# Attention branch c: two items a step on TensorE, the pair's second item normalised ahead of the next pair's maximum, the gate's products moved by half a chunk

## The reference, cut to what matters

```python
def block(args):
    qn, qp = args
    sc = (jnp.einsum('bqhd,bkhd->bhqk', qn, k_nope) + jnp.einsum('bqhd,bkd->bhqk', qp, k_pe)).astype(jnp.float32) * scale
    p = jax.nn.softmax(sc, axis=-1).astype(v.dtype)
    return jnp.einsum('bhqk,bkhd->bqhd', p, v)
...
branches = jnp.stack([oa, ob, oc], axis=2)
proj = jnp.einsum('bsnw,nwd->bsnd', branches, w_branch[l])
gates = jax.nn.sigmoid(h @ w_gate[l] + b_gate[l]).reshape(b, s_len, N_BRANCH, D_MODEL)
x = x + jnp.sum(gates * proj, axis=2) @ w_out[l]
```

## Time and profile before

| | us |
| --- | --- |
| median of 3 runs | 4201.57 |
| lowest and highest | 4198.54 and 4201.68 |
| the profiled execution's own time | 4204.7 |
| its span, first to last instruction | 4202.9 |
| branch c in layer 1, first score to the projection's second matmul | 2414.82 to 2506.14 |
| TensorE busy over the span | 3970.8 (94%) |
| VectorE busy over the span | 2298.5 (55%) |
| mean granted clock of TensorE | 0.981 |

### The profile page before, as it was taken

How to read it: one execution, slowest core, us unless ns; L and a number is a source line. 1 busy time by engine, 2 the same in 40 slices (tenths; PEclk the granted TensorE clock), 3 DMA queues, 4 the chain that set the end, 5 groups by cost and what they waited for, 6 DMA issues and landing times.

```text
span 4202.9 us, 52035 instructions
## 1 busy us (share of the span) xinstructions
PE 3970.8 (94%) x17600; PEld 2864.4 (68%) x17600; DVE 2298.5 (55%) x4427; ACT 1439.5 (34%) x3092; POOL 2201.4 (52%) x2879
## 2 busy tenths in 40 slices
PE   9999988887779999989999999999999999999998
PEld 7877633333336666679867768888888867768887
DVE  8376887887866666565375434321331375444321
ACT  3142322222245444445243323322332143323322
POOL 7646643333333333357835637556665735637654
PEclk9999999899899999999999999999999999999999
DMA  5342799999999999965412213333333312313332
GB/s 148 87 112 71 312 427 427 426 427 427 414 426 423 403 424 425 426 228 178 128 41 71 91 48 103 97 93 100 95 97 94 99 41 71 96 46 105 95 95 75
DMA packets 190865, 839.69 MB, mean 200 GB/s; under 512 B 41744, under 2 KB 44480, under 8 KB 125120
## 3 DMA queue, kind: packets, MB, share of 16 engines
q0 software_dynamic: 73728, 536.90, 30.4%
q1 hardware_dynamic: 91904, 293.46, 22.2%
q10 hardware_dynamic: 25024, 6.69, 0.8%
HBM read 831.47 MB, written 4.59 MB: 199 GB/s over the span
## 4 chain that ended last, share of the span: by engine, by line
PE 71%; DMA 13%; DVE 9%; ACT 2%; issue 2%; POOL 2%; DVEq 1%; ACTq 0%; POOLq 0%; SPq 0%
PE bank L953 17%; PE bank L955 17%; PE bank L954 17%; PE bank L1352 8%; DMA rows_o<-in_peer_uv,of_picks_int 4%; DMA row_keys<-in_peer_uv,of_picks_int 2%; DMA rows_x<-in_peer_uv,of_picks_int 2%; POOL wl L780 1%; DVE rows_o L2807 1%; PE bank L1047 1%; DMA work<-in_peer_uv,of_picks_int 1%; DMA rows_w<-in_peer_uv,of_picks_int 1%; DMA row_norm<-in_peer_uv,of_picks_int 1%; PE bank L1385 1%; DMA row_temps<-in_peer_uv,of_picks_int 1%
## 5 line engine op out<-in xcount | busy, mean ns | idle before, releaser
L780 POOL TENSOR_TENSOR wl<-raw,wh 128x256 fp32r<-128x256 f32 (+1 forms) x1032 | 824.7, 830 | 256.4 <-ACT wh L2067 232.1
L953 PE MATMUL bank<-xh,wh 128*128 128x512 f32 (+1 forms) x2304 | 881.3, 383 | 3.3 <-POOL wl L780 3.3
L955 PE MATMUL bank<-xh,wl 128*128 128x512 f32 (+1 forms) x2304 | 862.9, 375 | 0.0
L954 PE MATMUL bank<-xl,wh 128*128 128x512 f32 (+1 forms) x2304 | 862.4, 374 | 0.0
L780 POOL TENSOR_TENSOR wl<-raw_more,wh 128x256 fp32r<-128x256 f32 (+1 forms) x780 | 612.1, 816 | 286.5 <-ACT wh L2067 276.0
L953 PEld LDWEIGHTS bank<-xh,wh 128*128 128x128 f32 x2304 | 434.6, 189 | 105.8 <-issue 28.3
L955 PEld LDWEIGHTS bank<-xh,wl 128*128 128x128 f32 x2304 | 434.6, 189 | 79.3
L954 PEld LDWEIGHTS bank<-xl,wh 128*128 128x128 f32 x2304 | 435.1, 189 | 74.1 <-issue 2.2
L1352 PE MATMUL bank<-rows_o,diag 128*128 128x512 f32 x676 | 330.1, 623 | 48.0 <-ACT diag L2023 47.8
L2865 DVE TENSOR_TENSOR work<-bank,rstd 128x512 f32<-128x512 f32 (+1 forms) x184 | 114.8, 626 | 443.0 <-PE bank L955 442.4
L840 POOL DMA_INDIRECT rows_o<-in_peer_uv,of_picks_int x169 | 167.5, 991 | 288.5 <-PE bank L1352 277.6
(11 more groups left out here) (585 smaller groups left out, 8005.9 us busy)
## 6 DMA issues: line engine op xcount, KB each, us to landing
raw_more<-in_w_l SPq DMA_DIRECT2D x186, 512.0 KB
raw<-in_w_l SPq DMA_DIRECT2D x182, 512.0 KB
raw<-in_w SPq DMA_DIRECT2D x54, 512.0 KB
raw_more<-in_w_l SPq DMA_DIRECT2D x40, 448.0 KB
raw<-in_w_l SPq DMA_DIRECT2D x40, 448.0 KB
raw_more<-in_w_l SPq DMA_DIRECT2D x28, 256.0 KB
raw<-in_w_l SPq DMA_DIRECT2D x28, 256.0 KB
raw<-in_w SPq DMA_DIRECT2D x20, 256.0 KB
```

The source lines that it names most:

```text
L780: last = gp.tensor_tensor(wl[:, slot, c], source[:, c], f32(wh[:, slot, c]), ALU.subtract)
L953: pe.matmul(out, wh[:, slot, c], ah, start=k == 0, stop=False)
L954: pe.matmul(out, wh[:, slot, c], al, start=False, stop=False)
L955: mm = pe.matmul(out, wl[:, slot, c], ah, start=False, stop=k == last)
```

## The change

TensorE's loop takes a pair at a step. Step t has, in this order: turning item 2t-2; the scores of items 2t and 2t+1; the values product, for t = 4, 5, 8, 9; turning item 2t-1; the second half of gate chunk t-1; the first half of gate chunk t. VectorE normalises the odd item of a pair before it takes the next pair's first maximum, where it did so behind it; the rest of its loop is as it was. ScalarE's, GpSimd's and SyncE's programs are unchanged. No instruction is added or taken away: TensorE has 10426 rows and VectorE 2659 in the list of both kernels.

```diff
-                for s in range(18):
-                    if s < 16 and s % 2 == 0:
-                        h, qb = item_c(s)
-                        if s > 1:
-                            pe.wait_ge(exp_ready.sem, exp_ready.at(48 + s, l))
+                def turn_c(i):
+                    pe.wait_ge(prob_ready.sem, prob_ready.at(48 + i + 1, l))
+                    turn_tile(work[:, i % 4, :], l)
+                def values_c(h, turns):
+                    wait_total(l)
+                    pe.wait_ge(turn_read.sem, turn_read.at(t_base + turns, l))
+                    for b in range(NB):
+                        mm = pe.matmul(total[:], vt[:, b, h * P:(h + 1) * P], pt_c[h % 2][:, b, :], start=b == 0, stop=b == NB - 1)
+                    mm.then_inc(summed.sem, 1)
+                for t in range(10):
+                    if 1 <= t <= 8:
+                        turn_c(2 * t - 2)
+                    if t < 8:
+                        h, qb = item_c(2 * t)
+                        if t > 0:
+                            pe.wait_ge(exp_ready.sem, exp_ready.at(48 + 2 * t, l))
                         for m in range(2):
                             pe.matmul(score[m][:], qk[:, h + m, qb * P:(qb + 1) * P], qk[:, 6 + h + m, :], start=True, stop=False)
...
-                    if s < 16:
-                        linear(AT_L["gate_c"], s // 2, l, normed, share=(s % 2, 2))
-                    if s >= 8 and s % 8 < 2:
-                        h = 2 * (s // 8 - 1) + s % 8
-                        wait_total(l)
-                        pe.wait_ge(turn_read.sem, turn_read.at(t_base + s - 1, l))
...
-                    if 1 <= s <= 16:
-                        pe.wait_ge(prob_ready.sem, prob_ready.at(48 + s, l))
-                        turn_tile(work[:, (s - 1) % 4, :], l)
+                    if t in (4, 5, 8, 9):
+                        values_c(2 * (t // 4 - 1) + t % 4, 2 * t - 1 if t % 4 == 0 else 2 * t - 2)
+                    if 1 <= t <= 8:
+                        turn_c(2 * t - 1)
+                    if 1 <= t <= 8:
+                        linear(AT_L["gate_c"], t - 1, l, normed, share=(1, 2))
+                    if t < 8:
+                        linear(AT_L["gate_c"], t, l, normed, share=(0, 2))
...
                 for s in range(18):
+                    if 2 <= s and s % 2 == 0 and s <= 16:
+                        normalise(48 + s - 1, l, (s - 1) % 4, T, False)
                     if s < 16:
                         dve.wait_ge(scored.sem, scored.at(64 + s + 1, l))
...
-                    if 1 <= s <= 16:
+                    if s % 2 == 1 and s < 16:
                         normalise(48 + s - 1, l, (s - 1) % 4, T, False)
```

More of the change, by code:

```diff
@@ L1591, in _ @@
                                       start=False, stop=True).then_inc(scored.sem, 1)
-                    if s < 16:
-                        linear(AT_L["gate_c"], s // 2, l, normed, share=(s % 2, 2))
-                    if s >= 8 and s % 8 < 2:
-                        h = 2 * (s // 8 - 1) + s % 8
-                        wait_total(l)
-                        pe.wait_ge(turn_read.sem, turn_read.at(t_base + s - 1, l))
-                        for b in range(NB):
-                            mm = pe.matmul(total[:], vt[:, b, h * P:(h + 1) * P], pt_c[h % 2][:, b, :], start=b == 0, stop=b == NB - 1)
-                        mm.then_inc(summed.sem, 1)
-                    if 1 <= s <= 16:
-                        pe.wait_ge(prob_ready.sem, prob_ready.at(48 + s, l))
-                        turn_tile(work[:, (s - 1) % 4, :], l)
+                    if t in (4, 5, 8, 9):
[6 more added lines that the diff above has]
+                        linear(AT_L["gate_c"], t, l, normed, share=(0, 2))
                 t0 = use["total"] - 4
```

## The result

The changed kernel takes 4206.85 us, the median of 14 runs (4202.53 to 4216.6), against 4201.32 of the kernel before, run beside it 14 times. The ratio is 1.0015, 95% interval [1.0008, 1.0021]: 5.5 us slower. That is within the 0.2% that the prediction called no change, but it is clear of the noise of these runs, as the interval does not reach 1. The profiled execution took 4210.13 us for a span of 4208.3.

The account below looks back on a forecast made before the run. TensorE's own work was taken to bound the kernel. The terms -1.0, +0.7, +0.2, +2.45 and -1.3 sum to +1.05 us a layer, +2.1 in all, giving 4203.7 us; range 4199 to 4209.

Parts of the forecast that it names:

- The likeliest case: Whole kernel: the summed terms hold, +2.1 us with some tenths either way, no measurable change; chance 0.52.
- fewer runs, 7 pairs: TensorE's gate matmuls in branch c: one run of 24 replaces two of 12, -0.14 us a pair, -1.0 a layer.
- turnings slip: Branch c: normalising meets GpSimd's tile split, so TensorE's turning comes 0.17 us later in 4 steps, +0.7 a layer.
- first step: First pair of branch c: only half a chunk covers normalising item 0, so its turning waits, +0.2 us a layer.
- gap: Step 5: TensorE waits to turn item 9, whose normalising stands behind head_out of head 1, +2.45 us a layer.
- end: End of branch c: the last half chunk covers the wait before head 3's values, -1.3 us a layer.
- The chain at the end of a step: VectorE's gate sum, second maximum and normalising of item 2t precede TensorE's turning; meeting GpSimd makes normalising 0.80 us, +0.7 a layer.
- The whole-operation wait: Rival: VectorE's normalising waits until GpSimd's operation ends, +1.0 us a layer more, 4205.7 us; chance 0.12.
- The clock: Rival: TensorE's clock falls behind the new gap in one layer or both, 1.6 us each, 4205.3 or 4206.9; chance 0.18.
- Matmuls 0.43 apart behind the gap: Sign that would show the forecast wrong: TensorE's matmuls at this spacing after the wait in step 5, meaning the clock.
- The chain that sets the step: Rival: gate sum, maximum and normalising on VectorE decide each step's length, 0.45 us over 14 steps, 4210 us; chance 0.08.

Follow-up runs that it names:

- e3_whole_chunks: Against the changed kernel, each step issues both halves of its own gate chunk, without the shift by half a chunk; 4205.61 us, ratio 1.0013 to the kernel before.
- e1_norm_first: Against the changed kernel, VectorE normalises item 9 ahead of head_out of head 1; 4200.63 us, ratio 0.9998 to the kernel before.
- e2_half_between: Against the changed kernel, the second half of gate chunk 4 runs between head 1's values product and turning item 9; 4199.32 us against 4200.3 for the kernel before.
- e4_old_dve: TensorE's order as in the changed kernel, VectorE's loop as in the kernel before; 4225.43 us against 4200.3 for the kernel before, ratio 1.0058.
- e9_changed_look: The changed kernel without an edit, profiled once more; single time 4205.75 us.
- e0_again: The changed kernel without an edit, timed again; 4207.11 us against 4201.14 for the kernel before, ratio 1.0011.
- e7_gap_longer: Against the changed kernel, VectorE normalises item 9 behind the maximum of item 10; 4209.45 us, ratio 1.0022 to the kernel before.

## Why the prediction was right in kind and short in size

No change that can be measured was forecast, 4203.7 us, and 4206.85 came out, inside the range. The likeliest case gave +2.1 us, the medians differ by 5.5. The 0.2% that the prediction took as what can be measured was too coarse: with 14 runs of each kernel the interval reaches 0.07% to either side, and the 5.5 us stand clear of it. The terms, measured in layer 1 where no clock fell:

| Term | Forecast | Measured | From |
| --- | --- | --- | --- |
| fewer runs, 7 pairs | -1.0 | -0.6 | 7 x (9.29 - 9.38) |
| turnings slip | +0.7 | +0.4 | 4 x (9.40 - 9.29) |
| step 5's turning of item 10 | none | +0.35 | run 5.86 against 5.57, turning 0.50 against 0.44 |
| first step | +0.2 | +0.15 | run of 12 2.96 against 2.87, turning 0.49 against 0.43 |
| values products right behind scores | none | +0.2 | 3.54 and 3.53 against 3.43 |
| gap | +2.45 | +2.4 | 5.89 against 3.53 |
| end | -1.3 | -1.3 | 6.87 - 2.73 against 5.48 |
| sum | +1.05 | +1.5 | whole stretch: 92.77 - 91.32 = 1.45 |

The row of the end goes from the turning of item 15 to the projection's second matmul; 2.73 are the 12 matmuls that now stand in between.

*Fewer runs.* A late and an early pair on the timeline:

```profile
2439.20 0.65 PE L1047 MATMUL bank<-ident,work 128*128 128x128 f32 x4
...
2448.60 0.66 PE L1047 MATMUL bank<-ident,work 128*128 128x128 f32 x4
...
2486.32 0.60 PE L1047 MATMUL bank<-ident,work 128*128 128x128 f32 x4
...
2495.61 0.60 PE L1047 MATMUL bank<-ident,work 128*128 128x128 f32 x4
```

The late pair takes 2495.61 - 2486.32 = 9.29 us where 9.24 was forecast and 9.38 was usual. The run that was dropped does give back its border, but turning directly behind the scores takes 0.05 more than turning between two halves: the saving is 0.09 a pair, not 0.14. This was the operation that the trace of before didn't hold. The forecast's own terms, 3.31 + 0.36 + 5.58 less 0.03, make 9.22, not the 9.24 that it gives.

*The chain at the end of a step.* The mechanism is as worked out. The pair from 2439.20 takes 9.40 against a forecast of 9.24 + 0.17 = 9.41, but so close a sum is luck: the pair without a slip takes 0.05 more than forecast, and the slip is 9.40 - 9.29 = 0.11, not 0.17. Its VectorE and GpSimd side:

```profile
2446.01 0.69 DVE L2877 TENSOR_TENSOR gates<-bank,rstd 128x512 f32<-128x512 f32 x1 [2.43 <-PE bank L955]
...
2447.52 3.16 POOL L780 TENSOR_TENSOR wl<-raw,wh 128x256 fp32r<-128x256 f32 x4
...
2447.68 0.86 DVE L2315 TENSOR_SCALAR work<-work,stat 128x512 f32<-128x512 f32 x1
```

The normalising takes 0.86 where 0.80 was taken. It meets the split as said, and `e3_whole_chunks` confirms that by moving the split away. GpSimd pays as well, 3.16 us for four operations instead of 2.78. Not foreseen was step 5, where VectorE is idle 0.45 before a maximum's scaling and the turning waits 0.17 more:

```profile
2475.88 0.15 DVE L3164 TENSOR_SCALAR stat<-stat 128x1 f32<-128x1 f32 x1 [0.45 <-issue]
2476.18 0.76 DVE L2315 TENSOR_SCALAR work<-work,stat 128x512 f32<-128x512 f32 x1
...
2476.99 0.66 PE L1047 MATMUL bank<-ident,work 128*128 128x128 f32 x4 [0.17 <-DVE work L2315]
```

It follows the gap in layer 1 and also stands in `e1_norm_first`, which has no gap; the row gives only "issue" as its cause, and it stays open. Because of it the turnings cost +0.8 in all, near the +0.7 of the forecast, for another reason than the one given.

*The whole-operation wait.* The normalising above starts 0.16 into GpSimd's first operation, which takes 0.74 and ends at 2447.52 + 0.74 = 2448.26. Had it waited for that and then run its 0.49, it would have ended at 2448.75; it ended at 2447.68 + 0.86 = 2448.54. By the rule of the Trainium skill, "SBUF — State Buffer", section "Who interferes with whom", the later engine is blocked for the other's whole instruction; the trace shows the collision, but a shorter one.

*The gap and the end* are right to 0.1 us in size and right in place and releaser, and `e1_norm_first` and `e2_half_between` close the gap from either side. The forecast called the order on TensorE a given; a version that moves one half chunk shows that it was a choice of the change.

*Which step failed.* The likeliest case priced the new gap at its own length alone. The clock was held as a rival, 0.18, argued down since neither wait of the branch's end (0.78 and 1.11 us) had lowered it. That argued from shorter gaps than the new one. Matmuls 0.43 apart behind the gap had been named as a sign of being wrong, and they are there in layer 2. The rival's mechanism is right in that layer, its price of 1.6 measures 1.53. It did not come in layer 1, and a second fall, 1.54 us at a place with unchanged code, was in no case at all; so it is luck that the rival's 4206.9, with falls in both gaps, lies so close to 4206.85. The two falls make 3.1 of the 3.4 us by which the forecast was short; the rest is what layer 1's terms fell short by (0.4), the values products behind the scores above all. The chain that sets the step didn't come; `e4_old_dve` shows what it is like when it does.

## What to carry to other kernels

When an operation is moved ahead of a maximum, look at what it now stands behind: here a copy-out that waits for the very engine which waits for the moved operation, and one exchange of the two is worth all that the change lost. Price a new gap on TensorE twice, once as idle time and once with the matmuls behind it at half clock, and look for falls in stages that the edit leaves alone: one of the two here was in such a stage. A shift that hides one wait can make two engines work on SBUF at once elsewhere; cutting only the last chunk hid the same wait without that.

## What the runs showed of the hardware

The granted clock depends on more than the gap in front of it. Gaps of 2.2 us brought a fall 4 times in 10, always in the same layer of the same kernel, 3.0 us 3 times in 4, 1.84 us in another stage 11 times in 14, and 1.4 to 1.6 us never in 12. In all four profiles of the changed kernel the falls of layer 2 were at the same places, while the one behind the 1.84 us was there in two of the four. Each fall in layer 2 costs about 1.5 us.

Why the same gap lowers it in layer 2 and not in layer 1, and why the end of branch b falls with it, no run here settles. The time since the program's first instruction doesn't decide it: behind a gap of 2.18 us that ended at 3726.97 the clock fell (`e9_changed_look`), behind one of 2.19 that ended at 3727.03 it didn't (`e3_whole_chunks`); and the pause of 0.47 us at the end of branch b ended at 3589.68 with a fall in `e0_again` and at 3589.64 without one in `e7_gap_longer`.

The time outside branch c varies from one execution to the next: layer 1's branch began anywhere from 2409.3 to 2418.7 us. So small differences are read from the stretches here, not from the times: `e1_norm_first` is 2.2 us shorter than the kernel before in the two stretches and 0.5 in its median, with an interval of about 4 us to either side.

When GpSimd and VectorE work on SBUF at once, both can be longer: 0.49 becomes 0.72 to 0.86 for most of the normalisings in layer 1 that meet it, and four operations of GpSimd 3.16 instead of 2.8. Not every meeting costs: a normalising at 2485.47 in the changed kernel began while GpSimd was splitting a tile (2484.88 to 2486.55) and took its 0.49.
